# A new order for the first products, for the stretch between mixer and experts, and inside an expert group, in a two-layer hybrid encoder

## Reference

```python
for layer in range(2):
    mod = silu(c) @ ada_w[layer] + ada_b[layer]
    sh_m, sc_m, g_m, sh_f, sc_f, g_f = split(mod, 6)
    h = rmsnorm(x, norm_mix_g[layer]) * (1 + sc_m) + sh_m
    m = attn_lru_mixer(h) if layer == 0 else s5_mixer(h)
    x = x + g_m * m
    h = rmsnorm(x, norm_ffn_g[layer]) * (1 + sc_f) + sh_f
    # of each token's group: gates of its two best experts, 0 for the others
    for e in range(16):
        y += gates[:, e:e+1] * ((silu(h @ w1[e]) * (h @ w3[e])) @ w2[e])
    x = x + g_f * y
return rmsnorm(x, final_g)
```

## Time and profile before

| | us |
|---|---|
| median of 3 runs (lowest, highest) | 942.29 (941.72, 944.27) |
| the profiled execution | 942.3 |
| its span, first to last instruction | 940.5 |
| PE busy | 842.9 (90%) |
| DVE, ACT, POOL busy | 294.2, 191.1, 168.4 |
| DMA | 285.32 MB, mean 303 GB/s |
| mean granted PE clock | 0.952 |

### The profile page before, as it was taken

The page is one execution under the profiler, slowest core; times in us unless marked ns, Lnnn a source line. Parts: engine busy times, 40 slices in busy tenths (PEclk is TensorE's granted clock), DMA queues, the critical chain, the costliest instruction groups (busy, mean ns, idle before and its releaser), DMA issues.

```text
span 940.5 us, 12765 instructions
## 1 busy us (share of the span) xinstructions
PE 842.9 (90%) x5229; PEld 460.6 (49%) x5230; DVE 294.2 (31%) x694; ACT 191.1 (20%) x310; POOL 168.4 (18%) x258
## 2 busy tenths in 40 slices
PE   2699999799999998999599998799998899999992
PEld 0367644565455463553456543444443554654641
DVE  1347432641131320311799411530000310412214
ACT  1313330421221311311500101320001212213111
POOL 3201009186343434400033100100000000000000
PEclk9799999689999999999889999699999899999997
DMA  9999999539999999996996882208775399999961
GB/s 307 345 382 284 343 384 357 192 108 400 393 400 402 391 400 401 391 393 250 388 376 232 325 293 101 80 5 297 289 255 194 103 398 391 397 397 392 392 241 69
DMA packets 126288, 285.32 MB, mean 303 GB/s; under 512 B 7092, under 2 KB 8388, under 8 KB 125992
## 3 DMA queue, kind: packets, MB, share of 16 engines
q1 hardware_dynamic: 119392, 276.83, 80.0%
q0 software_dynamic: 1984, 5.21, 2.0%
q10 hardware_dynamic: 4872, 2.72, 1.0%
HBM read 279.50 MB, written 5.24 MB: 303 GB/s over the span
## 4 chain that ended last, share of the span: by engine, by line
PE 80%; DMA 8%; DVE 5%; ACT 3%; SPq 2%; issue 2%; ACTq 1%; DVEq 0%
PE PS L1606 19%; PE PS L1625 13%; PE PS L1633 8%; PE PS L1649 7%; PE PS L1894 6%; PE PS L1609 6%; PE PS L1377 4%; PE PS L1352 4%; PE PS L1446 3%; DMA yg<-in_s_c_im 3%; DMA ring<-in_moe_w 2%; DMA work<-in_ada_w 2%; PE PS L1429 2%; PE PS L1879 2%; SPq L340 1%
## 5 line engine op out<-in xcount | busy, mean ns | idle before, releaser
L1625 PE MATMUL PS<-ring,work 128*64 128x512 f32 (+1 forms) x512 | 130.5, 597 | 6.2 <-ACT work L779 6.2
L1606 PE MATMUL PS<-ring,hT 128*64 128x256 f32 x896 | 109.0, 385 | 3.0 <-DMA ring<-in_moe_w 3.0
L1606 PE MATMUL PS<-ring,yg 128*64 128x256 f32 x896 | 106.6, 379 | 0.0
L1606 PEld LDWEIGHTS PS<-ring,hT 128*64 128x64 f32 x896 | 66.8, 138 | 40.9 <-issue 9.3
L1625 PEld LDWEIGHTS PS<-ring,work 128*64 128x64 f32 (+1 forms) x512 | 43.1, 143 | 85.5 <-issue 85.5
L1218 DVE TENSOR_TENSOR work<-work,PS 128x512 f32<-128x512 f32 x32 | 22.0, 688 | 195.0 <-PE PS L1606 147.2
L1633 PE MATMUL PS<-work,xhat 128*128 128x256 f32 (+1 forms) x256 | 76.3, 451 | 7.0 <-issue 7.0
L1606 PEld LDWEIGHTS PS<-ring,yg 128*64 128x64 f32 x896 | 67.6, 137 | 29.2 <-issue 0.2
L1222 DVE COPY yg<-PS 128x512 f32<-128x512 f32 x32 | 22.1, 691 | 180.5 <-PE PS L1625 180.5
L1649 PE MATMUL PS<-yg,grow 64*128 64x512 f32 (+1 forms) x256 | 70.1, 612 | 7.1 <-DVE yg L1222 7.1
L1633 PEld LDWEIGHTS PS<-work,xhat 128*128 128x128 f32 x256 | 48.7, 205 | 38.8 <-issue 21.7
(11 more groups left out here) (351 smaller groups left out, 966.9 us busy)
## 6 DMA issues: line engine op xcount, KB each, us to landing
ring<-in_moe_w SPq DMA_DIRECT2D x96, 2048.0 KB, 16.8
ring<-in_ada_w SPq DMA_DIRECT2D x20, 2048.0 KB, 14.9
work<-in_ada_w SPq DMA_DIRECT2D x4, 2048.0 KB, 13.9
ring<-in_s_glu_w SPq DMA_DIRECT2D x4, 2048.0 KB, 16.0
ring<-in_ab_w_in SPq DMA_DIRECT2D x3, 2048.0 KB, 21.3
ring<-in_ab_w_out SPq DMA_DIRECT2D x2, 2048.0 KB, 13.6
rot_tables<-work POOLq DMA_DIRECT2D x16, 256.0 KB, 5.8
ring<-rot_tables SPq DMA_DIRECT2D x2, 2048.0 KB, 10.7
```

Of the source, the lines that this page charges most:

```text
L1606: last = mm(dst[64 * u:64 * u + 64, 0:256], hg[k][:, e * P:e * P + 64], w[:, k, 256 * u:256 * u + 256], start=k == 0, stop=k == KD - 1)
L1625: last = mm(dst, heT[:, at:at + (64 if narrow else P)], w[:, c4, h * HALF:(h + 1) * HALF], start=c4 == 0, stop=c4 == KF - 1)
```

## The change

All of it is order; no product is added or left out.

- PE turns the parameter rows before adaLN tiles 2 and 3 instead of after them. The first projection's block k waits for hT tile k only. POOL's wait for `ada_used` 4 now stands ahead of the `gaw` loads.
- `ada_cols(1)` comes after mixer tile (0, 0), `gate_row(0)` after (0, 1).
- The loads of `Cn` go from ACT's queue to SP's, after the last early adaLN tile and ahead of the expert tiles, behind a wait for `pv_done` 6.
- `turn_tables(0, 4)` moves into `ffn(0)`, behind the router, into banks 0, 5, 2, 3; ACT's `table_evac(0, 4)` behind both exponentials; `gate_row(n)` on ACT ahead of them. Accumulator 1 of layer 0 (bank 5) opens last, behind `tab_evac` 4; layer 1 opens three ahead of `member_ready`, not two.
- POOL does `over_row(0)` ahead of the table products, not behind them.
- In a group the turn of he(0) stands between up(1)'s two products, those of he(1) and he(2) ahead of `spread`, that of he(3) (bank 0, copied to `heT3`, the place of he(2)) ahead of down(2); down(3) follows down(2) at once and writes banks 0 and 1; spread(2) and spread(3) come last.

```diff
@@ SP, GpSimd
+            sp_.wait_ge(S("pv_done"), 6)
+            for v, name in enumerate(("s5_c_re", "s5_c_im")):
+                for u in range(2):
+                    sp_.dma_start(Cn[:, v, :, u * 64:(u + 1) * 64],
+                                  a[name][0].rearrange("(k g) c p -> (g c) k p", k=KD)).then_inc(S("cn_in"), 16)
...
+            pool.wait_ge(S("ada_used"), ADA_FIRST)
             for v, name in enumerate(("ab_gate_a_w", "ab_gate_x_w")):
...
-            pool.wait_ge(S("ada_used"), ADA_FIRST)
...
+            over_row(0)
             for tab, c0 in ((G1, 3), (G0, 5)):
...
-            over_row(0)
@@ ACT, def ffn(L)
-                if L == 0:
-                    table_evac(0, 4)
-                else:
+                if L == 1:
                     s.activation(warm, ones[:, 0:1], ACT.Sqrt)
                 norm(n)
                 modulate(n)
+                gate_row(n)
                 act.wait_ge(S("lg_ready"), L + 1)
...
-                gate_row(n)
                 act.wait_ge(S("l2_ready"), L + 1)
                 s.activation(exp_2, mx2, ACT.Exp).then_inc(S("exp_ready"), 1)
+                if L == 0:
+                    table_evac(0, 4)
...
                     he_t(2)
+                    he_t(3)
                     y_out(2)
-                    he_t(3)
                     y_out(3)
@@ PE, start
             turn_x(0)
-            ada(2, ADA_FIRST)
             pe.wait_ge(S("rows_in"), 16 * (len(ROWS) + 2))
...
+            ada(2, ADA_FIRST)
             ada_cols(0)
-            hT_ready(0)
             loaded(pe, 0)
             for b in range(NB):
                 for k in range(KD):
+                    if b == 0:
+                        pe.wait_ge(S(("hT_act", "hT_dve")[k // 2 % 2]), k // 4 * 2 + k % 2 + 1)
@@ PE, def ffn(L)
-                open_acc(0)
-                open_acc(1)
+                for m in (0,) if L == 0 else (0, 1, 2):
+                    open_acc(m)
+                if L == 0:
+                    turn_tables(0, 4)
                 pe.wait_ge(S("member_ready"), L + 1)
...
-                open_acc(2)
-                open_acc(3)
+                for m in (2, 3) if L == 0 else (3,):
+                    open_acc(m)
+                if L == 0:
+                    pe.wait_ge(S("tab_evac"), 4)
+                    open_acc(1)
@@ PE, a group
                             product_up(bank[bk], e, u3(n0 + j), narrow, ...).then_inc(S(sem), 1)
+                            if e == 1 and bk == 0:
+                                pe.wait_ge(S("pt_act"), gi + 1)
+                                turned(0, narrow)
...
+                    def turned(e, narrow):
+
+                        pe.wait_ge(S("he_ready"), 1 + e0 + e + 1)
+                        turn_he(he[:, e % 2, :], narrow, 0 if e == 3 else 2).then_inc(S("heT_ps"), 1)
...
                         up(1, narrow)
+                        pe.wait_ge(S("pt_dve"), gi + 1)
                         down(0, narrow)
                         up(2, narrow)
+                        pe.wait_ge(S("y_act"), 1 + e0 + 1)
+                        turned(1, narrow)
+                        spread(0, narrow)
                         down(1, narrow)
                         up(3, narrow)
+                        pe.wait_ge(S("y_act"), 1 + e0 + 2)
+                        turned(2, narrow)
+                        spread(1, narrow)
+                        turned(3, narrow)
                         down(2, narrow)
                         down(3, narrow)
+                        spread(2, narrow)
                         spread(3, narrow)
```

More of the change, by code:

```diff
@@ L196, in build @@
         heT = w3(o, HALF); o += HALF
+        heT3 = he[:, 0, :]
         gfrow = w3(o, D); o += D
@@ L722, in _ @@
             s.activation(lr_t[:, :, :], lr_t[:, :, :], ACT.Sqrt).then_inc(S("lru_a"), 1)
[L723 to L726, removed]
             rows_out(1)
@@ L778, in he_t @@
                         act.wait_ge(S("heT_ps"), e0 + e + 1)
-                        s.activation(heT[:, :], bank[2], ACT.Copy).then_inc(S("heT_ready"), 1)
+                        s.activation(heT3 if e == 3 else heT[:, :], bank[0 if e == 3 else 2], ACT.Copy).then_inc(
+                            S("heT_ready"), 1)
                     def y_out(e):
                         act.wait_ge(S("y_ps"), e0 + e + 1)
-                        s.activation(yg[:, e % 2, 0:HALF], bank[2], ACT.Copy).then_inc(S("y_act"), 1)
+                        s.activation(yg[:, e % 2, 0:HALF], bank[0 if e == 3 else 2], ACT.Copy).then_inc(S("y_act"), 1)
                     for k in range(0, KD, 2):
@@ L1221, in y_out @@
                         dve.wait_ge(S("y_ps"), e0 + e + 1)
-                        v.tensor_copy(yg[:, e % 2, HALF:], bank[3]).then_inc(S("y_dve"), 1)
+                        v.tensor_copy(yg[:, e % 2, HALF:], bank[1 if e == 3 else 3]).then_inc(S("y_dve"), 1)
                     for k in range(1, KD, 2):
@@ L1574, in _ @@
                 mix_out(b, h, LT, KD)
+                if (b, h) == (0, 0):
+                    ada_cols(1)
                 if (b, h) == (0, 1):
-                    ada_cols(1)
-                if (b, h) == (1, 0):
                     gate_row(0)
@@ L1586, in turn_tables @@
                     if n_ == 2:
-                        pe.wait_ge(S("grow_ready"), 1)
+                        pe.wait_ge(S("grow_ready"), 2)
                     if n_ == 7:
@@ L1594, in turn_tables @@
                     last.then_inc(S("tab_ps"), 1)
-            turn_tables(0, 4)
             pe.wait_ge(S("x_new"), 1)
@@ L1610, in product_up, with turn_he, product_down @@
                 return last
-            def turn_he(src, narrow):
+            def turn_he(src, narrow, dst=2):
                 for c4 in range(2 if narrow else 4):
-                    last = tr(bank[2][:, c4 * P:(c4 + 1) * P], src[:, c4 * P:(c4 + 1) * P])
+                    last = tr(bank[dst][:, c4 * P:(c4 + 1) * P], src[:, c4 * P:(c4 + 1) * P])
                 return last
-            def product_down(w, narrow):
+            def product_down(w, narrow, left=heT, to=2):
                 steps = [(h, c4) for h in range(2) for c4 in range(KF)]
@@ L1623, in product_down @@
                     at = (c4 % 2) * P + (c4 // 2) * 64 if narrow else c4 * P
-                    dst = bank[2 + h][64 * h:64 * h + 64, :] if narrow else bank[2 + h]
-                    last = mm(dst, heT[:, at:at + (64 if narrow else P)], w[:, c4, h * HALF:(h + 1) * HALF],
+                    dst = bank[to + h][64 * h:64 * h + 64, :] if narrow else bank[to + h]
+                    last = mm(dst, left[:, at:at + (64 if narrow else P)], w[:, c4, h * HALF:(h + 1) * HALF],
                               start=c4 == 0, stop=c4 == KF - 1)
@@ L1658, in ffn @@
                     pe.wait_ge(S("small_in"), 16 * 9)
-                    pe.wait_ge(S("tab_evac"), 4)
                 for k in range(KD):
@@ L1749, in down @@
                         pe.wait_ge(S("heT_ready"), 1 + e0 + e + 1)
-                        product_down(u3(n0 + j, D), narrow).then_inc(S("y_ps"), 1)
+                        if e < 3:
+                            last = product_down(u3(n0 + j, D), narrow)
+                        else:
+                            last = product_down(u3(n0 + j, D), narrow, heT3, 0)
+                        last.then_inc(S("y_ps"), 1)
                     def group(narrow):
```

12 lines of the change are left out of this document (1 added, 11 removed).

## The result

The changed kernel took 916.67 us (median of 4 runs, 915.16 to 918.34) beside 942.0 before: a ratio of 0.9726, with a 95% interval from 0.9701 to 0.9752. That is 25.3 us; the forecast said 20.2 (922.1). The low end of its range, 917.0, lies 0.3 us above the median and inside the interval (913.8 to 918.6 by the ratio), so whether the result falls in or out of the range is within the noise; the 5 us to the forecast itself are not. The profiled execution took 917.73, with a span of 916.0 and a mean clock of 0.956.

What follows compares the result with a forecast made beforehand. TensorE and DMA were both taken as bounds of the expert groups, the stream binding layer 0 and PE layer 1. 8.7 us before the experts (3.3 + 5.4) + 1.7 + 9.8 = 20.2 us, from 942.3 to 922.1; range 917 to 927.

Steps and rivals of the forecast that it cites:

- First products: Start up to the first projection: turns moved ahead, later gate loads and hT waits tile by tile save 3.3 us.
- Between mixer and experts: From mixer's end to xhat's turn (turn_x), layer 0: turn_x starts at 166.8 in place of 172.26, 5.4 us.
- rival (3): Layer 0's router: transposes keep the clock up, gather 8.10 not 10.21, openings 0.9 sooner; 3.0 us, 919.1; chance 0.22.
- one of the forecast's own signs of being wrong: Ahead of the gather: a wait for tab_evac or pick_ready would show the forecast wrong.
- DVE beside GpSimd: Group 0 of layer 0: DVE's picks beside table building may be slower by 0 to 3 us, hidden by slack.
- Layer 0's groups: Layer 0's experts: 9.8 us of stalls go, but the DMA stream lets only 1.7 arrive; end at 438.4.
- Layer 1's groups: Layer 1's experts: 4 x 2.45 = 9.8 us of removed stalls arrive whole; at worst 1 is lost.
- The S5 stretch: Between layer 0's experts' end and xhat's turn for layer 1's experts: forecast step 0.
- case (6): SP's queue: the c loads hold it and PE waits for an expert tile; slower, 945.3; chance 0.02.
- Cases (2): Layer 0's groups: DMA does not hold them, 9.8 us gained and not 1.7; 914.0; chance 0.03.
- (4): Layer 0's router: openings at half clock, 1.9 later, gather or turn_x 2 us worse; 926.0; chance 0.11.
- (5): Expert groups: each stall turns up at the next instruction, only 8.7 us is left; 933.6; chance 0.04.

Runs made afterwards that it cites:

- the changed kernel's second profile: The changed kernel run again unaltered, beside the second set of runs: 917.47 us, ratio 0.9727.
- fill_fitted: Changed kernel plus 4, 6, 1 and 2 identity products without a reader in TensorE's waits before the norms and wide gathers: 913.4 us, ratio 0.969.
- group_only: Kernel before with only the new order inside an expert group: 928.36 us, ratio 0.9843.
- over_row_back: Changed kernel with GpSimd's over_row put back behind the table building: 919.71 us, ratio 0.9759.
- split_tables: Changed kernel with GpSimd's table G1 built ahead of over_row and G0 behind it: 914.53 us, ratio 0.9698.
- all_fitted: Changed kernel plus tables split around over_row, fitted identity products in waits, and two at the wide body's end: 909.74 us, ratio 0.9656.

## Why the prediction was right and wrong

**First products**, 3.3 forecast, 4.2 measured (4.2 alone). The term "0.7 us from a full stream, which the tile gains" was too small: the gate loads held the tile back by 1.8 to 2.1 us, above even my upper bound of 1.5. The turns and evacuations gave their 1.13, and hT 1.37 where 1.46 was written. The first projection started at 35.77, not at 37.7. Some 1.1 us of that is the clock's: the fourth tile's product took 2.57 instead of 3.64. The projection gave it back, partly at half clock, 16.48 us instead of 15.40.

**Between mixer and experts**, 5.4 forecast, 5.3 measured: the chain (residual behind PE's last tile, 2.81 us from norm to turn, nothing of ACT ahead of it) is right to 0.1 us. The three openings (six instructions) took 2.84, as they do at full clock, which is rival (3) for that part; but of its 3.0 us only 0.8 came. PE then waited 1.18 us for DVE's one-hot `pick`, one of the forecast's own signs of being wrong, and the gather behind it ran half cold again. In the changed kernel's second profile the same openings took 4.64, no wait followed, and 0.4 us was gained: the clock falls at another point in each profile. The clock, rows of windows in the changed kernel (openings, then the gather's first part):

```profile
174.50:177.30 2.80, 2.80 (x7) 1.04 (x7) 2.49 (x15) 1.97 (x3) 0.70 (x3) 1.00 0.00 1
177.40:184.10 6.70, 5.55 (x13) 4.50 (x14) 1.79 (x8) 0.83 (x2) 6.20 (x16) 0.50 0.00 1
```

The openings of fill_fitted, behind which PE had no idle time at all:

```profile
173.10:175.70 2.60, 2.60 (x7) 1.03 (x6) 2.30 (x13) 1.92 (x3) 0.54 (x3) 1.00 0.10 35
```

PE was busy all through the openings, and the clock fell to 0.50, the 1.2 GHz level, right behind them; in fill_fitted it fell in the last opening, with no idle time before it. The Trainium skill ("TensorE: Matmul & The Clock Gate", Part 1) has the gate follow how busy PE has been. The runs bear out one half: full-size products in the wait for the residual kept the clock. The other half they don't: one-row openings did not, though the profile counts PE as busy throughout. Which kinds of work hold the clock no run here sorts out, as turns and narrow products stand before the openings too.

**DVE beside GpSimd**, "slower, by 0 to 3 us", hidden by the group's slack. Measured, 7 us for one set of eight, and PE waited 3.18 us in group 0 and 4.2 in group 3. From first up product to its end the layer took 248.0 to 251.5 us in the six profiles with the new group and these waits, and 247.0 to 247.5 in the four where the tables stand elsewhere (group_only, over_row_back, split_tables, all_fitted). The contention cost some 2 us by the means; with the old group 4.6 were lost. Only part of it was hidden. The bound of 3 was too low because I took it for a slower DVE, not for a queue behind GpSimd's instructions of over 1 us. The rotation tables, the other thing that came later, cost nothing: their last product ended at 395.2, and 399.4 was forecast.

**Layer 0's groups**, 1.7 forecast, 1.1 measured; end 437.4 against 438.4. Without the contention the term holds: 2.0 in group_only, 2.2 with split tables. That the weight stream bounds this layer is right: its last tile landed at 430.0 (431 forecast), 237.1 us behind the first issue, 236.3 before, group_only turned 7 of its 9.8 into waits for tiles, and all_fitted has 12.4 us of them. The ring waits came to 4.4 in the changed kernel, not 5 to 8 (and 3.0 of them were there before), since the picks' waits took their share.

**Layer 1's groups**, 9.8 forecast, 13.3 measured (12.7 with the group alone, 12.5 in the changed kernel's second profile). This is the step that failed, as a term too small: "2.45 us of PE a group", which "arrive whole". Each group's three stalls did go, so the mechanism was right. But what was counted was only their idle time. In the wide group the third stall lay inside the 9.1 us behind DVE's copy and was worth nothing; instead a spread of 3.5 us moved into that time. Two stalls 1.6, spread 3.5, and 0.2 from 9.30 to 9.10 make 5.3, as measured. The match to 0.1 is in part luck: behind the gather the group is 5.6 shorter, and the gather itself took 0.3 longer. I had read the issue gap only where it stood ahead of the wide gather (2.18) and costed it at nothing. In the narrow groups each removed stall also gives back an overlap: two down products in one run took 7.09 where two runs of 3.65 sum to 7.30, and two spreads 3.70 where two of 1.99 sum to 3.98. With the 2.45 that makes 2.9 of the 3.0 to 3.2. This sum is read from the rows; no run takes one overlap away alone. The last group gave 1.8, not 2.45: the stream caught it, with 0.8 us of waits for tiles. The forecast had named such waits as a sign of being wrong, and its "at worst 1 is lost" allowed for them.

**The S5 stretch**, 0 forecast, 1.0 lost (143.0 us between the marks, 142.0 before). It took 141.5 in the changed kernel's second profile and 142.1 with the gate loads early, so it varies from run to run, and nothing shows it to be the change's.

**Slower**, case (6): the c loads on SP's queue delayed nothing. The four took 16.1 us to issue (121.4 to 137.5), not 28, and in the expert groups PE waited for no tile ahead of group 2 (counted from 0). Cases (2), (4) and (5) are out by the rows above. The terms that were too small sum to 3.5 (layer 1) + 0.9 (start) + 0.8 (clock); those too large to 0.6 (layer 0) + 1.0 (S5), and the span's tail gave 0.6 more. So the miss is smaller than the errors in it: terms 5.2 us too small stand against 1.6 too large.

## What to carry to other kernels

A stall is worth its idle time plus the overlap that its neighbours regain; but ahead of a jump to another body, only what stands before the last blocking wait counts, and work moved behind that wait is free as long as it fits into the jump's own time (9.1 us here). When GpSimd's work is moved, lay its instructions beside DVE's one by one: any order blocks something, and it should be something with slack. Waits of TensorE a few us long may be worth filling, but only up to their length. And a mark read from one profile of each kernel can be off by more than the term in question: read it in every run that shares the code.

## What the runs showed of the hardware

- DVE's 128x128 pick with two pointer operands took 0.3 us alone and 1.2 beside GpSimd's 128x512 tensor products, one for one; a norm pass of 1.22 took 2.18. An operation that reads PSUM kept its 0.81.
- From DVE's last copy in a wide body, for which PE waits, to the first product of the narrow body 9.1 to 9.5 us passed in twelve profiles, with 3.7 to 8.6 us of PE's work in that time; 11.0 passed in the one where the work was longer than that.
- Gate loads in runs of 256 bytes, 262 KB in all, delayed a 2.1-MB tile by 1.8 to 2.1 us.
- Three one-row openings (six instructions) filled PE's time and did not hold its clock: it was at 1.00 in them and at 0.50 right behind. Four identity products of full size in a wait of 4.3 us held it (xhat's turn 1.94 us instead of 2.71). With a fifth behind the openings, itself at half clock, the gather went from 10.55 to 8.66 us.
